# Differential attention of a two-block transformer kernel: one wait split in two, one copy and five weight splits moved

## What is computed

```python
q = apply_rope(q, cos, sin)          # [1, 512, 8 heads, 2 components, 64]
k = apply_rope(k, cos, sin)
s = jnp.einsum('bqhcd,bkhcd->bhcqk', qb, k) * HEAD_DIM ** -0.5
s = jnp.where(kpos <= qpos, s, NEG_INF)
p = jax.nn.softmax(s, axis=-1)
a = p[:, :, 0] - lam * p[:, :, 1]
o = jnp.einsum('bhqk,bkhe->bqhe', a, v)
```

## Time and profile before

| | |
|---|---|
| median of 3 runs | 1990.58 us (1989.1 to 1990.81) |
| profiled execution | 1989.57 us, its span 1987.8 us |
| PE busy | 1962.2 us, 99% |
| DVE, ACT, POOL busy | 1029.9, 805.4, 269.6 us |
| granted clock of PE | 0.999 of full speed |
| attention stage | about 1088 to 1186 us of the span |

### The profile page before, as it was taken

The page is one execution under the profiler, slowest core; times in us unless marked ns, Lnnn a source line. Parts: engine busy times, 40 slices in busy tenths (PEclk is TensorE's granted clock), DMA queues, the critical chain, the costliest instruction groups (busy, mean ns, idle before and its releaser), DMA issues.

```text
span 1987.8 us, 25222 instructions
## 1 busy us (share of the span) xinstructions
PE 1962.2 (99%) x10000; PEld 1662.0 (84%) x10000; DVE 1029.9 (52%) x1575; ACT 805.4 (41%) x1466; POOL 269.6 (14%) x280
## 2 busy tenths in 40 slices
PE   8999999999999999999999999999999999999998
PEld 7888988888888888888988788888888888888887
DVE  6765665555354222333563768877765543222333
ACT  5542543334343222333333873566663342222332
POOL 1001000000000000000003542477860000000000
PEclk9999999999999999999999999999999999999999
DMA  6331333333323333332453144211225323333332
GB/s 213 106 100 56 112 107 102 98 96 96 96 88 107 101 98 96 96 96 85 122 151 114 50 149 148 73 61 49 64 78 198 112 79 110 98 96 95 96 96 74
DMA packets 60100, 201.68 MB, mean 101 GB/s; under 512 B 8304, under 2 KB 8336, under 8 KB 59600
## 3 DMA queue, kind: packets, MB, share of 16 engines
q1 hardware_dynamic: 56080, 185.10, 30.0%
q0 software_dynamic: 3904, 14.97, 2.2%
HBM read 180.64 MB, written 8.39 MB: 95 GB/s over the span
## 4 chain that ended last, share of the span: by engine, by line
PE 92%; DVE 3%; ACT 2%; POOL 1%; issue 1%; DVEq 1%; DMA 1%; POOLq 0%; ACTq 0%; SPq 0%
PE ps L691 27%; PE ps L689 27%; PE ps L690 27%; PE ps L1203 1%; PE ps L1241 1%; PE ps L1240 1%; PE ps L1183 1%; PE ps L1184 1%; PE ps L781 1%; PE ps L1110 1%; POOL PU L645 1%; DVE XN L1874 1%; PE ps L867 1%; ACT XN L1357 0%; PE ps L845 0%
## 5 line engine op out<-in xcount | busy, mean ns | idle before, releaser
L1834 DVE TENSOR_TENSOR Wl<-raw,Wh 128x1024 fp32r<-128x1024 f32 x307 | 378.3, 1235 | 688.9 <-ACT Wh L1324 687.5
L689 PE MATMUL ps<-HTh,Wh 128*128 128x512 f32 (+1 forms) x1712 | 641.4, 375 | 2.1 <-DVE gst L2416 1.2
L691 PE MATMUL ps<-HTh,Wl 128*128 128x512 f32 (+1 forms) x1712 | 636.8, 372 | 0.0
L690 PE MATMUL ps<-HTl,Wh 128*128 128x512 f32 (+1 forms) x1712 | 636.5, 372 | 0.0
L1324 ACT CAST Wh<-raw 128x1024 fp32r<-128x1024 f32 x307 | 321.7, 1051 | 736.1 <-DMA raw<-in_w_all 736.1
L691 PEld LDWEIGHTS ps<-HTh,Wl 128*128 128x128 f32 x1712 | 322.4, 188 | 56.3
L689 PEld LDWEIGHTS ps<-HTh,Wh 128*128 128x128 f32 x1712 | 322.6, 188 | 55.8 <-issue 2.1
L690 PEld LDWEIGHTS ps<-HTl,Wh 128*128 128x128 f32 x1712 | 322.7, 189 | 53.3
L689 PE MATMUL ps<-Wh,Yh 128*128 128x512 f32 x528 | 205.8, 390 | 0.0
L691 PE MATMUL ps<-Wh,Yl 128*128 128x512 f32 x528 | 205.5, 389 | 0.0
L690 PE MATMUL ps<-Wl,Yh 128*128 128x512 f32 x528 | 205.4, 389 | 0.0
(11 more groups left out here) (287 smaller groups left out, 2265.6 us busy)
## 6 DMA issues: line engine op xcount, KB each, us to landing
raw<-in_w_all SPq DMA_DIRECT2D x307, 512.0 KB, 3.5
swp_d<-qkd SPq DMA_DIRECT2D x64, 64.0 KB, 2.8
g_dram<-gst SPq DMA_DIRECT2D x16, 256.0 KB, 3.8
ring<-g_dram POOLq DMA_DIRECT2D x16, 256.0 KB, 3.5
X<-in_x SPq DMA_DIRECT2D x4, 512.0 KB, 6.2
swp_r<-qkr SPq DMA_DIRECT2D x16, 128.0 KB, 3.6
gpre<-in_g_pre POOLq DMA_DIRECT2D x4, 512.0 KB, 3.9
Kh<-Kh SPq DMA_DIRECT2D x16, 128.0 KB, 2.3
```

The costliest lines, as they stand in the source:

```text
L689: tensor.matmul(dst, a_hi, b_hi, start=start, stop=False)
L690: tensor.matmul(dst, a_hi, b_lo, start=False, stop=False)
L691: return tensor.matmul(dst, a_lo, b_hi, start=False, stop=stop)
L1834: vector.tensor_tensor(Wl[:, s, :], raw[:, s, :], Wh[:, s, :], ALU.subtract).then_inc(w_lo, 1)
```

## The change

Four edits. (1) PE waits for three of a head's four parts ahead of component 0's first scores, and for all four ahead of component 1's; the twin wait stays ahead of both. (2) ACT's `nsf_out` stands behind `da_out` and `turned_out` of its step, no longer ahead of them. (3) ACT's five weight splits inside the attention move from t = 1, 5, 9, 17, 25 to 17, 21, 25, 27, 29. (4) DVE's move from t = 5, 9, 13, 21, 29 to 18, 22, 26, 28, 30. The chunks are those of nst (three) and the first two of rope_q, in the same order.

```diff
--- before.py
+++ after.py
@@ -379,8 +379,8 @@
 
         TWIN_AT = {CHUNK0["vda"] + 4: (0,), CHUNK0["vda"] + 7: (1,), CHUNK0["nsf"]: (2, 3), CHUNK0["nsf"] + 1: (4, 5),
                    CHUNK0["nsf"] + 2: (6, 7)}
-        HIGH_AT = (1, 5, 9, 17, 25)
-        LOW_AT = (5, 9, 13, 21, 29)
+        HIGH_AT = (17, 21, 25, 27, 29)
+        LOW_AT = (18, 22, 26, 28, 30)
 
         def qk_parts(head):
 
@@ -834,10 +834,11 @@
                 w = width(t)
                 q = slice(i * P, (i + 1) * P)
                 if t % 4 == 0:
-                    pe.wait_ge(st_lo, qk_parts(t // 4) + 4)
                     pe.wait_ge(k_twin[u], 32 * (t // 8) + 32)
                 for m in range(2):
                     b = b2 + m
+                    if t % 4 == 0:
+                        pe.wait_ge(st_lo, qk_parts(t // 4) + 3 + m)
                     bank_free("da", b, t // 2)
                     dst = ps[b][:, 0:w]
                     if m == 1:
@@ -1509,11 +1510,11 @@
                 exps(0)
                 exps(1)
                 for t in range(TOTAL):
-                    if nsf_ends(t) is not None:
-                        nsf_out(nsf_ends(t))
                     if exists(t - 2):
                         da_out(t - 2)
                     turned_out(t)
+                    if nsf_ends(t) is not None:
+                        nsf_out(nsf_ends(t))
                     head = t // 4 + 2
                     if exists(t + 2):
                         exps(t + 2)
```

## The result

The changed kernel takes 1992.67 us (median of 22 runs, 1991.91 to 1993.88) against 1989.45 us for the kernel before (22 runs beside it, 1989.1 to 1990.93). The ratio is 1.0015, 95% interval 1.0009 to 1.0021: slower by 3.2 us. The time lies inside both ranges given, the difference above the forecast's own +0.5 to +2.2. The profiled execution took 1993.20 us with a span of 1991.4, 3.6 more than before.

The account below looks back on a forecast made before the run. PE, busy 99% of 1987.8 us, bounds the kernel; only 4.4 us of attention idle time was winnable. Terms -3.03 + 0.30 + 1.32 + 1.03 + 1.83 = +1.45, taken as +1.4 on 1990.58: 1992.0 us, range 1987.6 to 1994.6.

Parts of the forecast that it names:

- the sum: Differential attention: gains of 3.03 us against costs of 0.30, 1.32, 1.03 and 1.83, in all +1.45 us, taken as +1.4.
- rival B: Head starts: component 1 or ACT's relay holds the turn, only head 3's 0.61 is won, splits cost 4.18; +3.6 us, chance 0.12.
- -3.03 + 0.30 + 1.32 + 1.03: Up to head 7: earlier starts win 3.03 us; heads 2 to 4 lose 0.30, splits in heads 5 and 6 cost 1.32 and 1.03.
- Rival A: DVE behind a head's first scores: slack covers the splits, early starts stay whole; about -3.0 + 0.3 us, 1987.9, chance 0.20.
- Two terms that were put at nothing: ACT's moved split halves cost nothing; the key product copy ahead of exps(20) and exps(29) costs 0 to 0.1 us, taken as 0.
- the sum had 1.83: Last head: DVE splits at t=26 and t=28 cost 0.70 and 1.13 us, together 1.83.
- From turn(29) on PE has nst tiles to fill every gap: End of the stage: the split at t=30 and the missing one at 29 cost nothing; later stages give nothing back.
- Part 1: Head starts: component 0 waits for three parts; heads 2 and 4 to 7 win 0.54, 0.54, 0.39, 0.55 and 0.40 us.
- part 3: Weight splits: removed DVE halves win only POOL's 0.15 us; new places at t%4 = 2 fall whole on the loop.
- the earlier S: S is PE's start of a head's first scores; DVE's first maxima, 0.84 us later, were said to profit, DVE being idle.
- The shared operands: DVE and POOL share a port pair, second blocks: Kl ends 1.12 us behind the split, turn 6.78 us after the head's start.

Follow-up runs that it names:

- e7_copy_back: The changed kernel with edit 2 undone (key product copy ahead of da_out again): 1992.90 us against 1989.89 for the kernel before.
- e6_high26: The changed kernel with one ACT split half moved from t=27 to t=26: 1992.94 us against 1989.89 for the kernel before.
- e2_wait_copy: The kernel before with edits 1 and 2 only, all weight splits in their old places: 1989.01 us against 1989.55 for the kernel before.
- e5_low29: The changed kernel with one DVE split half moved from t=28 to t=29: 1990.33 us against 1989.89 for the kernel before.
- e8_fill: The changed kernel with one of the two nst tiles of t=29 ahead of turn(29) on PE: 1990.15 us against 1989.89 for the kernel before.
- e1_wait: The kernel before with edit 1 alone (the wait split in two): 1989.54 us against 1989.55 for the kernel before.
- e3_splits: The kernel before with edits 3 and 4 alone (weight splits moved): 1994.85 us against 1989.55 for the kernel before.
- e12_nowait: The kernel before with edit 2 and all five weight splits off the loop, without edit 1: 1988.64 us against 1989.77 for the kernel before.
- e13_kl_first: Edits 1 and 2, splits off the loop, one nst tile ahead of turn(29), POOL order Kh 0, Kl 0, Kh 1, Kl 1: 1986.30 us against 1989.77 before.
- e10_loopfree: The kernel before with edits 1 and 2 and all five weight splits off the loop: 1987.36 us against 1989.77 for the kernel before.

## Why the prediction was right, and where it was not

**Direction and place: right, the time with luck.** Same within 0.2% was given 0.92, and the change is +0.15% (3.2 us). The predicted time, 1992.0, is 0.7 us from the measured one, but the difference misses by 1.8 us (+1.4 for +3.2): the sum was put on the median of three runs (1990.58), 1.1 us above that of 22 (1989.45), and this hides over half of the miss. By number the result is nearer to rival B (+3.6), whose mechanism did not occur. The range's lower end does not follow from its own words either (1987.9 less 1.0 is 1986.9, not 1987.6); nothing hung on it.

Up to head 7 the starts went as described. There the sum said -0.38 us (-3.03 + 0.30 + 1.32 + 1.03), and the profile has -0.36. Turn to start is 4.20 in the kernel after, start to turn 5.84 to 5.85 without a split (forecast 5.85), 6.75 and 6.76 with one (forecast 6.78), because Kl stood behind the split in just the way that was worked out. Rival A (splits covered) and rival B (component 1 held) are out: no start of the kernel after waits for POOL.

**The end: 0.4 us short.** Two terms that were put at nothing fail together at t=27: "The ACT halves stand between exps and a da_out that waits for PE in either order: nothing" and, for the kraw copy that edit 2 puts ahead of exps(29), "between 0 and 0.1 us, taken as 0". The copy makes exps(29) late, the ACT half behind it follows late, and DVE's split stands still for it (0.43 us). From head 7's start to turn(29) two splits cost 10.00 - 7.75 = 2.25 us, where the sum had 1.83. Either cure is worth 0.5 us: e7_copy_back, with the copy back ahead, takes 9.51 (1.76 for the two splits), e6_high26, with the ACT half earlier, takes 9.47. With no ACT half behind it the copy is free: e2_wait_copy takes 7.74.

**The clock: 1.5 us missing.** "From turn(29) on PE has nst tiles to fill every gap, so ... no later stage gives anything back" is true of the gaps and left out the pace. With the 0.4 us at the end it makes up the difference: 1.45 + 0.42 + 1.51 = 3.4 us, where 3.2 were measured. e5_low29 and e8_fill, two ways to shorten the idle time, end 2.8 and 3.0 us under the changed kernel, each against the kernel before.

**The reason for the gain: wrong for each edit, although their sum was right.** Part 1 booked 0.4 to 0.55 us per head to the split wait, and part 3 said of the removed splits "Taking them away wins nothing but POOL's 0.15 us". e1_wait won nothing (0.3 us in the stage), e2_wait_copy 0.5 us, not 3.0. The sentence of part 1 that fails is "DVE can use the earlier S": DVE's first maxima could, but its second combine was bound to POOL's Kl, Kl to the Kh copies, and these to combine(t) behind the split and behind Qst. I had costed this path only for the kernel after, where heads 2 to 4 have no split in it. From turn to turn heads 2 and 4 show the two shares and what they make together:

| turn to turn, heads 2 and 4 | splits in their old places | no split in these heads |
|---|---|---|
| all four parts awaited | 10.49 (before) | 10.34 (e3_splits) |
| edit 1 | 10.50 (e1_wait) | 10.05 (after) |

The wait alone wins nothing, the splits alone win just the 0.15 us that the prediction gave them, and both together 0.44, which is also what the sum had for such a head (0.54 less 0.10). So the sum was right for the two edits together, and wrong in what it says of each: the 0.54 of part 1 can be had only when the split is gone, and with part 1 in place taking the split away wins far more than 0.15. e12_nowait agrees: without edit 1 start to turn is 5.72, PE's own limit, and the loop 10.35, and in head 5, where one nsf step is missing and start to turn is 5.41, it is 10.05 with the wait split or not. So with edit 1 the loop is POOL's, beside a split (10.50) and without one (10.05; 9.92 in e13_kl_first, which changes nothing but POOL's order). Before, both paths ended at the same time, and taking PE's wait away uncovered the other. Over the whole stage the splits' way out of the loop was worth 1.9 us on top of edits 1 and 2 (e2_wait_copy to e10_loopfree, each against the kernel before), and edit 1 was worth 1.3 us with the splits out (e12_nowait to e10_loopfree).

**The shared operands: right.** In the kernel after Kl is the second to come (2.17 us in place of 1.27), in e3_splits the split is (2.10 in place of 1.22), in e13_kl_first neither collides. The order, by tenths of a microsecond, decides who pays. These rows agree with the Trainium skill (SBUF — State Buffer, section Who interferes with whom), by which the second instruction blocks until the first ends. The agreement is to 0.2 us: Kl takes 1.27 us alone and ends 1.11 behind the split, and in e3_splits the split takes 1.22 alone and ends 1.08 behind Kl. And the recorded starts do not always tell the order: in e2_wait_copy combine(15) starts 0.02 us ahead of Kl and is still the one that pays.

## What to carry to other kernels

A wait at the head of a loop shows which path ends last, not by how much: before booking its length as a gain, follow the second path from the last common point, here through POOL, and cost it with the old neighbours still in place. Work that must lie somewhere in a tight loop costs least where its engine already waits for another (here 0.45 us a head behind t%4 = 1, and 0.90 behind t%4 = 2); outside the loop, in the idle time ahead of it, it cost nothing. And idle time of PE at the end of a stage can cost twice, since the clock may fall behind it.

## What the runs showed that I had not expected

- Waits of PE of 3.1 us in all between 1167 and 1174 us (0.33, 0.75, 0.67, 1.32) were followed by 3.4 us at a granted clock of 0.53 to 0.61, worth 1.5 us. With 1.75 us of waits (e5_low29, e8_fill) nothing fell. With 2.6 us the traces of e6_high26 and e3_splits show no fall and that of e7_copy_back shows one. In e3_splits PE is as little busy in the 4 us before turn(29) as in the changed kernel (1.20 and 0.68 us of 2.00). A single wait as long as 1.77 us (head 5 of e3_splits) was followed by none. What tells these apart stays open.
- The same 1024 column subtraction took 1.22 us in one order of issue and 2.10 us in another, with Kl's 2.17 us as the mirror image.
